# Mixing output of a decoder layer: two weight slots split into an early part and a late part

## What is computed

```python
    qm, km, vm, qg, kg, vg, gg, log_a = mixer_projections(h, pos, w_mix_in, w_gk_up, b_gk)
    o_moba = moba_fn(qm, km, vm)
    o_gla, s_fin = gla_chunked(qg, kg, vg, log_a, gla_s0, gla_chunk)
    o_gla = gla_output(o_gla, gg, gla_norm_g, x.dtype)
    mix = jnp.concatenate([o_moba, o_gla], axis=-1) @ w_mix_out
    x = post_norm_residual(x, mix, m[:, 5], 1.0, ln_g[1], ln_b[1])
```

## Time and profile before

| | us |
|---|---|
| median of 3 runs | 979.55 |
| the three runs | 981.81, 979.55, 974.18 |
| the profiled execution | 972.42 |
| its span, first to last instruction | 970.4 |
| TensorE busy | 910.6 (94%) |
| VectorE busy | 549.1 (57%) |
| ScalarE busy | 359.8 (37%) |
| matmuls of `pair_slot` on `Hh`, `wh` (L695) | 274.2, 912 times |
| matmuls of `values` (L940) | 29.5, idle before them 18.2 |

### The profile page before, as it was taken

One profiled execution on the slowest core, in us unless ns is written; L12 is line 12 of the kernel. 1 busy time (PEld: TensorE's weight loads), 2 busy tenths in 40 slices (PEclk: granted clock), 3 DMA queues, 4 the chain that ended last, 5 costly groups with the idle time before them and its releaser, 6 DMA issues.

```text
span 970.4 us, 17321 instructions
## 1 busy us (share of the span) xinstructions
PE 910.6 (94%) x6987; PEld 793.3 (82%) x6987; DVE 549.1 (57%) x846; ACT 359.8 (37%) x510; POOL 28.0 (3%) x34
## 2 busy tenths in 40 slices
PE   6999999999999999999798998849899999989997
PEld 2688888988998689996577876639679999989994
DVE  0635544455664786876753457614666665654655
ACT  1533332233332555445743345411333332323334
POOL 0000000000000000000000000001200000000100
PEclk9999999999999999999798899978999999999999
DMA  9999888986556744439399599997415555434511
GB/s 329 302 299 260 243 226 249 259 238 159 149 150 214 242 148 134 158 114 322 114 324 386 182 345 385 385 347 217 129 35 141 153 151 144 134 93 132 153 43 54
DMA packets 214885, 199.93 MB, mean 206 GB/s; under 512 B 9569, under 2 KB 161261, under 8 KB 214678
## 3 DMA queue, kind: packets, MB, share of 16 engines
q1 hardware_dynamic: 213412, 194.99, 64.7%
q0 software_dynamic: 704, 2.49, 0.7%
q10 hardware_dynamic: 690, 1.35, 0.4%
HBM read 195.00 MB, written 3.80 MB: 205 GB/s over the span
## 4 chain that ended last, share of the span: by engine, by line
PE 36%; SPq 7%; DVE 3%; issue 2%; DMA 2%; ACT 2%; DVEq 0%; ACTq 0%
PE B L695 9%; PE B L696 9%; PE B L700 9%; SPq L623 6%; PE B L891 2%; DMA ring<-in_cache_v 1%; PE B L795 1%; PE B L940 1%; PE B L1022 1%; PE B L902 1%; SPq L606 1%; DMA W<-in_cache_v 1%; PE B L922 1%; ACT Z L1237 0%; DVE rstd L1696 0%
## 5 line engine op out<-in xcount | busy, mean ns | idle before, releaser
L695 PE MATMUL B<-Hh,wh 128*128 128x320 f32 x912 | 274.2, 314 | 0.6 <-issue 0.6
L696 PE MATMUL B<-Hl,wh 128*128 128x320 f32 x912 | 270.5, 310 | 0.0
L1580 DVE TENSOR_TENSOR wl<-raw,wh 128x2048 fp32r<-128x2048 f32 x90 | 207.3, 2304 | 89.0 <-ACT wh L1237 88.8
L1237 ACT ACTIVATE wh<-raw 128x2048 fp32r<-128x2048 f32 x90 | 172.2, 1913 | 147.1 <-PE B L700 114.4
L695 PEld LDWEIGHTS B<-Hh,wh 128*128 128x128 f32 x912 | 172.3, 189 | 10.7 <-issue 10.0
L696 PEld LDWEIGHTS B<-Hl,wh 128*128 128x128 f32 x912 | 172.4, 189 | 0.3
L700 PE MATMUL B<-Hh,wl 128*128 128x320 f32 x912 | 152.7, 310 | 0.0
L700 PEld LDWEIGHTS B<-Hh,wl 128*128 128x128 f32 x912 | 139.0, 188 | 0.0
L695 PE MATMUL B<-Gh,wh 128*128 128x320 f32 x352 | 105.1, 313 | 2.5 <-DVE Gl L1708 2.5
L696 PE MATMUL B<-Gl,wh 128*128 128x320 f32 x352 | 104.8, 312 | 0.0
L1237 ACT ACTIVATE sg<-B 128x320 f32<-128x320 f32 x46 | 20.1, 437 | 212.8 <-PE B L700 196.9
(11 more groups left out here) (247 smaller groups left out, 968.2 us busy)
## 6 DMA issues: line engine op xcount, KB each, us to landing
raw<-in_w_ffn_in SPq DMA_DIRECT2D x88, 512.0 KB, 6.2
raw<-in_w_ada SPq DMA_DIRECT2D x72, 512.0 KB, 5.0
ring<-in_cache_k SPq DMA_DIRECT2D x96, 256.0 KB, 4.8
ring<-in_cache_v SPq DMA_DIRECT2D x96, 256.0 KB, 6.0
raw<-in_w_ffn_out SPq DMA_DIRECT2D x32, 384.0 KB, 3.4
raw<-in_w_mix_in SPq DMA_DIRECT2D x24, 512.0 KB, 4.8
raw<-in_w_ffn_out SPq DMA_DIRECT2D x32, 320.0 KB, 4.1
M<-in_cache_v SPq DMA_DIRECT2D x16, 256.0 KB, 4.9
```

Of the source, the lines that this page charges most:

```text
L695: pe.matmul(out, w, xh[k], start=start and k == 0, stop=False)
L696: pe.matmul(out, w, xl[k], start=False, stop=False)
L1237: return act.activation(out, in_, func, **kw)
L1580: dve.tensor_tensor(wl[:, wbuf(n), :], raw_view(n), f32(wh[:, wbuf(n), :]), ALU.subtract).then_inc(lo_ready, 1)
```

## The change

- `early_slot(k)` runs slot k (0 or 1) of the mixing output ahead of the end of the sample attention: chunks 4 to 7 with all 320 columns, chunks 0 to 3 with the 256 columns of the prompt. The sums stay open. Slot 0 stands before `values(3, 0, 2)`, slot 1 before `values(3, 1, 1)`.
- `late_slot(k)` computes what was left out, for 64 columns and 4 chunks, with the tokens as the stationary operand: 12 matmuls of a 128 x 64 piece of `Hh` or `Hl` against 256 columns of weights, out 64 x 256. VectorE copies it to `arow`, and `turn_late(k)` adds it, turned, into the open sums by two matmuls with the identity.
- The banks of slots 0 to 3 are now 0/1, 3/4, 5/6 and 0/1. The low part of slot 1 goes to a free part of `Gh` instead of `wl` (whose second buffer shares its memory with `PT`).
- SP loads slot 0 ahead of page group 56 and slot 1 ahead of group 59.
- VectorE forms the low part of slot 1 before the last heads are scaled. It waits for `mo_whole` in place of `used` before the residuals of slots 0 and 1, and forms those of slots 2 and 3 one step earlier.

```diff
 A1, F1, O1, A2, MI, MO, F2, O2, END = 0, 8, 52, 68, 74, 86, 90, 112, 128
 MI_TILES = [0, 1, 2, 3, 6, 7, 4, 5, 8, 9, 10, 11]
+
+EARLY_SLOT = (2, 1)
+MO_BANKS = [0, 3, 5, 0]
 READ = {"F1": 1, "O1": 23, "MI": 31, "MO": 43, "F2": 47, "O2": 69}
...
         OB = 2
+        low_mo = Gh[:, :, :].rearrange("p c n -> p (c n)")[:, SLOT:2 * SLOT]
+
         def split_view(t, n, kind):
             v = t[:, wbuf(n), :]
+            if n == MO + 1 and t is wl:
+                v = low_mo
             if kind == "ffn_in":
                 return v.rearrange("p (a k f) -> p a k f", a=2, k=KT)
             if kind == "wide":
...
             if b == IN_W:
                 return W[:, 512 * j:512 * j + 512]
             return ring[:, 4 * b + j, :]
+
+        def late_out(k):
+            return (B[OB], tb(("pick", NPAIR - 1)))[k][0:NS, 0:256]
         def tb(key):
...
         tp_filled, tp_act, tp_dve = sem("tp_filled"), sem("tp_act"), sem("tp_dve")
         s_out, own_ready, bias_ready, exp_done = sem("s_out"), sem("own_ready"), sem("bias_ready"), sem("exp_done")
         rinv_ready, v_used, pv_out, om_ready = sem("rinv_ready"), sem("v_used"), sem("pv_out"), sem("om_ready")
+        late_copied, mo_whole = sem("late_copied"), sem("mo_whole")
         o_hi, s_act, s_dve = sem("o_hi"), sem("s_act"), sem("s_dve")
         y_T, y_act, y_dve, y_stored, stored = sem("y_T"), sem("y_act"), sem("y_dve"), sem("y_stored"), sem("stored")
         MEAN, VAR = B[7][:, 0:N], B[3][:, 0:N]
...
                 load_wide(At(MI + n), mix_in, 256 * MI_TILES[n])
             sp.wait_ge(s_pg, 16)
             for n in range(len(PAGE_GROUPS)):
-                if n in (len(PAGE_GROUPS) - 4, len(PAGE_GROUPS) - 2):
-                    k = 0 if n == len(PAGE_GROUPS) - 4 else 1
-                    load_wide(At(MO + k), mix_out, 256 * k)
+                for k in range(2):
+                    if n == len(PAGE_GROUPS) - 8 + 3 * k:
+                        load_wide(At(MO + k), mix_out, 256 * k)
                 load_pages(n)
             for k in range(2, 4):
                 load_wide(At(MO + k), mix_out, 256 * k)
...
                         high, low = [vh[:, k, fs] for k in range(KT)], [vl[:, k, fs] for k in range(KT)]
                     m = product(B[b0 + h][:, 0:N], t, high, low, xh, xl, True, True, h == 1)
                 m.then_inc(used, 1)
+
+            def early_slot(k):
+
+                t = At(MO + k)
+                vh, vl = split_view(wh, t.n0, "wide"), split_view(wl, t.n0, "wide")
+                parts = [(c, 0, N) for c in range(HP, KT)] + [(c, 0, S) for c in range(HP)]
+                wait_high(t)
+                for h in range(2):
+                    for c, lo, hi in parts:
+                        out, w = B[MO_BANKS[k] + h][:, lo:hi], vh[:, c, h * P:(h + 1) * P]
+                        pe.matmul(out, w, Hh[:, c, lo:hi], start=(c == HP), stop=False)
+                        pe.matmul(out, w, Hl[:, c, lo:hi], start=False, stop=False)
+                wait_low(t)
+                for h in range(2):
+                    for c, lo, hi in parts:
+                        pe.matmul(B[MO_BANKS[k] + h][:, lo:hi], vl[:, c, h * P:(h + 1) * P], Hh[:, c, lo:hi],
+                                  start=False, stop=False)
+
+            def late_slot(k):
+
+                t = At(MO + k)
+                vh, vl = split_view(wh, t.n0, "wide"), split_view(wl, t.n0, "wide")
+                out = late_out(k)
+                for c in range(HP):
+                    pe.matmul(out, Hh[:, c, S:N], vh[:, c, :], start=(c == 0), stop=False)
+                    pe.matmul(out, Hl[:, c, S:N], vh[:, c, :], start=False, stop=False)
+                    m = pe.matmul(out, Hh[:, c, S:N], vl[:, c, :], start=False, stop=(c == HP - 1))
+                m.then_inc(used, 1)
+
+            def turn_late(k):
+
+                pe.wait_ge(late_copied, k + 1)
+                for h in range(2):
+                    m = pe.matmul(B[MO_BANKS[k] + h][:, S:N], arow[0:NS, k, h * P:(h + 1) * P], ident[0:NS, 0:NS],
+                                  start=False, stop=True)
+                m.then_inc(mo_whole, 1)
             def hidden_slot(t, half, bank):
...
                             own_scores(i + 1)
                         turn_keys(i + 1, j, 0)
                         turn_keys(i + 1, j, 1)
+                    if i == NPAIR - 1 and j == EARLY_SLOT[0]:
+                        pe.wait_ge(go_done, 1)
+                        wait_dve(("po", HP - 1))
+                        early_slot(0)
                     values(i, 0, j)
                     if i + 1 < NPAIR:
                         if j < 2:
                             point(m0 + 2 + j)
                         scores(i + 1, j)
             for g in range(4):
+                if g == EARLY_SLOT[1]:
+                    early_slot(1)
                 values(NPAIR - 1, 1, g)
             pick_heads(NPAIR - 1)
-            pe.wait_ge(go_done, 1)
             wait_dve(("pick", NPAIR - 1))
-            for k in range(4):
-                if k >= 2:
-                    pe.wait_ge(out_read, READ["MO"] + k - 1)
-                pair_slot(At(MO + k), "wide", 2 * (k % 2))
+            late_slot(0)
+            late_slot(1)
+            turn_late(0)
+            turn_late(1)
+            pair_slot(At(MO + 2), "wide", MO_BANKS[2])
+            pe.wait_ge(out_read, READ["MO"] + 1)
+            pair_slot(At(MO + 3), "wide", MO_BANKS[3])
             norm_mean(1)
             norm_var(1)
             keep_busy(B[2], 12)
...
                 dve.wait_ge(hi_ready, t(split_through))
                 if before_refill(n):
                     dve.wait_ge(used, before_refill(n))
-                dve.tensor_tensor(wl[:, wbuf(n), :], raw_view(n), f32(wh[:, wbuf(n), :]), ALU.subtract
+                dst = low_mo if n == MO + 1 else wl[:, wbuf(n), :]
+                dve.tensor_tensor(dst, raw_view(n), f32(wh[:, wbuf(n), :]), ALU.subtract
                                   ).then_inc(lo_ready, 1)
             def add_bias(bank, col, lo, hi):
...
                         if j < 3:
                             block_values(i + 1, j)
             low(At(MO))
+            low(At(MO + 1))
             own_heads(NPAIR - 1)
             out_low(NPAIR - 1)
-            low(At(MO + 1))
             dve.wait_ge(stored, STORED_MIX * 16)
+            for k in range(2):
+                dve.wait_ge(used, MO + k + 1)
+                dve.tensor_copy(arow[0:NS, k, :], late_out(k)).then_inc(late_copied, 1)
+            low(At(MO + 2))
             for k in range(4):
-                dve.wait_ge(used, MO + k + 1)
-                residual(2 * k, B[2 * (k % 2)], 5, False, None)
-                residual(2 * k + 1, B[2 * (k % 2) + 1], 5, True, READ["MO"] + k + 1)
-                if k < 3:
-                    low(At(MO + k + 2))
+                if k < 2:
+                    dve.wait_ge(mo_whole, k + 1)
+                else:
+                    dve.wait_ge(used, MO + k + 1)
+                residual(2 * k, B[MO_BANKS[k]], 5, False, None)
+                residual(2 * k + 1, B[MO_BANKS[k] + 1], 5, True, READ["MO"] + k + 1)
+                if k == 0:
+                    low(At(MO + 3))
+                if k == 2:
+                    low(At(F2))
             norm(1, lambda: low(At(F2 + 1)))
             modulate(2)
```

## The result

| | before | after |
|---|---|---|
| median of 4 runs each, us | 978.90 | 964.70 |
| lowest to highest | 974.18 to 981.81 | 961.64 to 969.34 |
| ratio after/before, 95% interval | | 0.9873 (0.9826 to 0.9921) |
| the profiled execution | 972.42 | 961.64 |
| its span | 970.4 | 959.6 |

Forecast were 970.2 for the median and 963.1 for the profiled execution.

What follows compares the result with a forecast made beforehand. Bytes bound the stretch up to 654 us, TensorE the one behind. Gained 16.6 less paid 7.3 saves 9.3 us: 963.1 for the profiled execution, median 970.2, range 964.5 to 976.

Steps and rivals of the forecast that it cites:

- Early slot 0: In the gap before `values(3, 0, 2)`: slot 0 runs 633.6 to 640.0, costs nothing and takes a slot from behind.
- The pages: Page groups between the moved loads land one place later, `values(3, 0, 3)` at 643.4; the last still land at 651.8 and 654.4.
- The queue was not held up: Sync engine's in-order queue: groups 62 and 63 go out about 641 and 644.5; cost nothing, at most 0.5 us.
- Early slot 1: Before `values(3, 1, 1)`: runs 648.0 to 656.1, 3.5 us of it at half clock, putting 2.4 us on the path.
- The clock: TensorE around the last page gaps: 1.2 GHz from about 644, back some 5.4 us after dense work begins at 646.1.
- the clock stays: Rival, chance 0.25: TensorE's clock stays or falls only shortly around the last page gaps; saved 12.1 us, median 967.4.
- First late matmul: After the last values at 659.2, heads' copy and pick put it at 661.1 for 659.2 before, 1.9 us paid.
- Late slots and turn: After the pick: two late slots of 1.4 us each, then a turn of about 0.7, ending 665.2; 4.1 us paid.
- slot 2's landing: Slot 2's weights go out at 658.1 and land at 664.4, so slot 2 starts at 666.4 after rounding.
- two slots and the slow start gone: Behind the attention: two slots of 7.04 us and 2.5 us of half-clock start disappear, 16.6 us gained.
- slot 2's wait: TensorE waits 1.2 us between the turn's end and slot 2's start, because slot 2's weights land late.
- slower: Rival, chance 0.04: late slot 0 weights delay `values(3, 0, 2)`, group 62 and the last pages; 3 us slower, 982.5.

Runs made afterwards that it cites:

- both edits: The change with early slot 1 before `values(3, 1, 0)` and VectorE's FFN 2 first-slot subtraction behind the norm's mean subtraction; median 963.51 us, ratio 0.9858.
- late part the usual way round: The change with late matmuls having weights stationary, 64 columns moving, straight into the open banks, no copies or turn; one run 980.52 us, stretch 61.61.
- subtraction moved: The change with VectorE's subtraction for FFN 2's first slot moved behind the norm's subtraction of the mean; one run 954.11 us, stretch 55.93.
- change again: The changed kernel once more, unaltered, against the kernel before; median of 6 runs 965.77 us, ratio 0.9888, stretch 58.30.

## Why the prediction held, and where a step was off

**Gained, by steps.** *Early slot 0*: forecast 633.6 to 640.0 with the values until 640.9; measured 633.92 to 640.51 with the values until about 641.6, no wait inside. Its 256-column matmuls go 8 in 0.96 us (635.20 to 636.16), 120 ns each: the choice of 118 over 147 was right. *The pages*: the forecast put `values(3, 0, 3)` at 643.4 and `values(3, 1, 0)` at 646.1; measured 644.25 and 646.94, 0.85 later each. *The queue was not held up*: the 20 ring transfers went out in one run, and TensorE found the last three groups there at 656.07. *Early slot 1*: 648.80 to 656.07, forecast 648.0 to 656.1.

**The clock.** Forecast at 1.2 GHz from about 644 to 651.5; measured 643.8 to 650.2. It was taken from the earlier trace rows, the pattern of one group in a gap, and it held. In all five executions with the change's early order it fell, in the 0.7 us ahead of the group of `values(3, 0, 3)` or between that group and the one of `values(3, 1, 0)`. The rival "the clock stays", 0.25, was not idle: it is what slot 1 one group earlier did in one of two executions. Where the Trainium skill (TensorE: Matmul & The Clock Gate, Why this matters for your kernels) blames idle gaps between bursts, the trace agrees that filled gaps keep the clock, in both experiments that filled them, but it also fell 3.2 us behind the last gap, of 0.57 us, under the 64-column matmuls, so gaps are not the whole of it.

**Paid.** *First late matmul*: forecast 661.1, measured 661.01. *Late slots and turn*: two late slots from 661.01 to 663.91, 2.9 us for the forecast 2.8. The turn takes 1.24 us rather than 0.7, since of the four small matmuls the second pair waits on VectorE's copy, which starts at 664.02; it ends at 665.15, forecast 665.2. The three small misses cancel.

**The term that was off: slot 2's landing.** I let its 1 MB land 6.3 us after issue, so that slot 2 would start at 666.4. It went out at 658.08, as forecast (658.1), and ScalarE had it at 663.20, after 5.1 us, within the 3.6 to 5.9 of the earlier trace rows which I had before me. The 6.3 is the forecast's own step from 653.80 to 660.1, the longest landing and some 0.4 us for the transfer issued behind the first. So slot 2 started at 665.16, right behind the turn, and the wait of 1.2 us was zero. That it is exactly zero is this execution's luck: over the six others where ScalarE waited for it, the load took 5.0 to 5.8 us, and TensorE's wait was up to 0.64.

**The wait I had not seen.** The forecast put the mean's start at 680.6 and it came at 680.41 (9.5 us saved up to there, for 9.3), but that close a hit is luck: two errors cancel, 1.2 us sooner by slot 2 and 0.9 later by GpSimd's sum. I had counted VectorE's work (13.95 us against 14.1) and not who runs beside it. It cost nothing, as the experiment without it shows, since the residual tiles are ready at the same place: the last mean matmul comes 16.9 us behind slot 2's start with it and without it. So 9.3 us up to the mean's start became 10.5 up to its last matmul, and the whole balance, measured to that last matmul, is

| | forecast, us | measured, us |
|---|---|---|
| two slots and the slow start gone | 16.6 | 16.5 (692.58 - 659.20, less 682.06 - 665.16) |
| later first late matmul | -1.9 | -1.8 |
| late slots and turns | -4.1 | -4.15 |
| slot 2's wait | -1.2 | 0 |
| rest | -0.1 | 0 |
| saved | 9.3 | 10.5 (692.58 - 682.06) |

and the profile's own time came out 961.64 for 963.1. The forecast's mechanism, with its steps, held; the one term that was mis-sized is slot 2's wait. Between the medians the difference is 14.2 us in that comparison and 11.2 in the second one (977.0 to 965.77). The forecast for the median, 970.2, was built on the 7.1 us by which the profiled execution lay below it; that scatter is not a property of the change, and in after's four runs the profiled one lies 3.1 below. That makes 4.1 of the 5.5 us between 970.2 and 964.7; the steps make 1.4. That the median still lay inside the range, by 0.2 us, owes something to luck.

**The rival "slower"** did not come; with the loads at their old place, its chain is there, and took 5.0 of the 10.8 us. The order of loads was the edit that prevented it.

**What stays open.** When exactly the clock falls. It had fallen when the group behind a gap of 2.66 us began (change), 2.44 (both edits), 2.21 (late part the usual way round) and 2.20 (subtraction moved). It had not behind gaps of 2.57 (change again), 2.23 (slot 2 loaded earlier) and 2.18 (slot 1 one group earlier); in the first two of these it fell at or before the next gap. And it fell under dense matmuls with 64 columns moving. So the length of the gap alone doesn't decide. No run here isolates what does, and whether slot 1 one group earlier is faster by more than the scatter is not settled.

## What to carry to other kernels

Where a stretch waits for bytes, a block of matmuls whose inputs are partly ready can be cut into a large part for the gaps and a small late part with the few tokens stationary; it is worth the block's time, plus what a restored clock gives behind, less the late part, and its weights must be loaded ahead of the data that the gaps wait for, or the block holds up the queue (5.0 of 10.8 us here). Judge such an edit by the distance between two fixed rows of the trace, and know how far that scatters (2.4 us here). Of a wait near the end of a stage ask first what else ends at that moment: in the change's own execution two of them (slot 2's load, GpSimd's sum) were covered, and nothing was gained without them, but other executions of the same order show them uncovered by 0.2 to 0.8 us.
